# Three modulation vectors by a fused multiply and sum on VectorE instead of TensorE

## What is computed

```python
def adaln_params(cond, w_mod, b_mod):
    m = jax.nn.silu(cond) @ w_mod + b_mod
    return jnp.split(m[..., None, :], N_MOD, axis=-1)     # N_MOD = 6, w_mod [1024, 6144] per layer
...
        sh1, sc1, g1, sh2, sc2, g2 = adaln_params(c, w_mod[l], b_mod[l])
        csh1, csc1, cg1, csh2, csc2, cg2 = adaln_params(c_ctx, w_mod[l], b_mod[l])
...
        hf = modulate(rms_norm_2(x, norm_ffn[l]), sh2, sc2)
        x = x + g2 * conv_ffn(hf, w_up[l], conv_w[l], w_down[l])
```

## Time and profile before

| | us |
|---|---|
| median of 3 runs (lowest to highest) | 2077.11 (2076.71 to 2077.42) |
| span of the profiled execution | 2074.6 |
| PE busy | 2052.7 |
| DVE busy | 1367.3 |
| ACT busy | 1101.8 |

### The profile page before, as it was taken

One profiled execution on the slowest core, in us unless ns is written; L12 is line 12 of the kernel. 1 busy time (PEld: TensorE's weight loads), 2 busy tenths in 40 slices (PEclk: granted clock), 3 DMA queues, 4 the chain that ended last, 5 costly groups with the idle time before them and its releaser, 6 DMA issues.

```text
span 2074.6 us, 36374 instructions
## 1 busy us (share of the span) xinstructions
PE 2052.7 (99%) x14782; PEld 1832.1 (88%) x14782; DVE 1367.3 (66%) x2356; ACT 1101.8 (53%) x1839; POOL 72.2 (3%) x55
## 2 busy tenths in 40 slices
PE   9999999999999999999999999999999999999998
PEld 9999999999999999997677887778888888999998
DVE  6687767567687677574464445665555667667786
ACT  5576576545676685553476233433332346645554
POOL 2210000000300000000000000000000000000000
PEclk9999999999999999999999999999999999999999
DMA  8556444566655545564223434433333343454552
GB/s 286 180 166 207 160 143 166 190 218 235 226 170 187 176 130 183 201 221 158 82 72 102 152 129 176 142 112 132 112 132 127 117 152 107 140 180 161 186 174 81
DMA packets 93511, 330.62 MB, mean 159 GB/s; under 512 B 10272, under 2 KB 13600, under 8 KB 93088
## 3 DMA queue, kind: packets, MB, share of 16 engines
q1 hardware_dynamic: 93344, 328.30, 46.3%
HBM read 327.08 MB, written 1.18 MB: 158 GB/s over the span
## 4 chain that ended last, share of the span: by engine, by line
PE 91%; DVE 5%; ACT 3%; issue 1%; DMA 0%; DVEq 0%; SPq 0%; ACTq 0%
PE ps L945 25%; PE ps L946 24%; PE ps L947 24%; PE ps L1028 2%; PE ps L958 1%; PE ps L959 1%; PE ps L960 1%; DVE t_lo L1684 1%; ACT t_hi L1354 1%; PE ps L1259 1%; PE ps L1101 1%; PE ps L1269 1%; PE ps L1280 1%; PE ps L1117 1%; PE ps L1082 1%
## 5 line engine op out<-in xcount | busy, mean ns | idle before, releaser
L945 PE MATMUL ps<-t_RB,t_hi 128*128 128x256 f32 (+1 forms) x3712 | 1163.3, 313 | 4.0 <-ACT t_MT L1400 1.4
L946 PE MATMUL ps<-t_RB,t_hi 128*128 128x256 f32 (+1 forms) x3712 | 1144.2, 308 | 0.0
L947 PE MATMUL ps<-t_RB,t_lo 128*128 128x256 f32 (+1 forms) x3712 | 1143.7, 308 | 0.0
L1684 DVE TENSOR_TENSOR t_lo<-t_raw,t_hi 128x1024 fp32r<-128x1024 f32 (+1 forms) x503 | 608.7, 1224 | 355.5 <-ACT t_hi L1354 354.2
L945 PEld LDWEIGHTS ps<-t_RB,t_hi 128*128 128x128 f32 x3712 | 707.9, 191 | 74.7 <-issue 25.2
L946 PEld LDWEIGHTS ps<-t_RB,t_hi 128*128 128x128 f32 x3712 | 708.3, 191 | 35.0 <-issue 1.9
L947 PEld LDWEIGHTS ps<-t_RB,t_lo 128*128 128x128 f32 x3712 | 708.1, 191 | 35.2
L1354 ACT ACTIVATE t_hi<-t_raw 128x1024 fp32r<-128x1024 f32 (+1 forms) x506 | 520.4, 1041 | 398.7 <-PE ps L947 369.9
L2124 DVE SCALAR_TENSOR_TENSOR t_A<-ps,t_V,t_A 128x510 f32<-128x510 f32 (+1 forms) x176 | 102.1, 611 | 89.3 <-ACT t_A L1644 87.8
L1644 ACT ACTIVATE t_A<-ps,t_V 128x512 f32<-128x512 f32 (+1 forms) x88 | 48.4, 576 | 127.3 <-PE ps L947 127.3
L2097 DVE SCALAR_TENSOR_TENSOR t_X<-ps,t_MOD,t_X 128x256 f32<-128x256 f32 x168 | 72.6, 477 | 32.7 <-PE ps L947 32.7
(11 more groups left out here) (304 smaller groups left out, 1893.3 us busy)
## 6 DMA issues: line engine op xcount, KB each, us to landing
t_raw<-in_W SPq DMA_DIRECT2D x586, 512.0 KB, 3.8
t_A<-cu_scratch SPq DMA_DIRECT2D x8, 512.0 KB, 5.7
t_B<-cu_scratch SPq DMA_DIRECT2D x8, 512.0 KB, 5.6
t_raw<-in_W SPq DMA_DIRECT2D x16, 256.0 KB, 3.0
t_A<-in_C SPq DMA_DIRECT2D x2, 1536.0 KB, 6.9
t_X<-in_X SPq DMA_DIRECT2D x2, 512.0 KB, 4.3
t_X<-in_X SPq DMA_DIRECT2D x1, 1024.0 KB, 7.5
out<-t_X SPq DMA_DIRECT2D x4, 256.0 KB, 2.5
```

What stands on the lines that cost most here:

```text
L945: mm(o, hi[:, w], xh(k), start=k == 0 and j == 0, stop=False)
L946: mm(o, hi[:, w], xl(k), start=False, stop=False)
L947: i = mm(o, lo[:, w], xh(k), start=False, stop=k == nkt - 1 and m == u.x[1] - 1)
L1684: tt(t.lo[s][:, 0:w], t.raw[r][:, 0:w], t.hi[s][:, 0:w].bitcast(F), ALU.subtract).then_inc(*up("dve", ("split", u.i)))
```

## The change

For the second layer of the second block, the last three vectors (j = 3, 4, 5, in 24 pieces of 128 outputs, numbered 24 to 47) are no longer made on PE. A new unit `condb` loads the two conditionings, each copied to all 128 partitions, into `t.CB` (tiles `t_T1` and `t_E`), and ACT applies silu to them. A new unit `modv` takes one load of 128x1024, in which a partition holds the 1024 input weights of one output, and runs two fused instructions on DVE, one for each conditioning: multiply by the row of the conditioning, sum along the row from the bias on, and write the sum to a column of `t_MOD`. The product itself goes to the scratch `t.CBO` in the first and over the weights in the second. `modv` follows each of the first 24 weight products of the first feed-forward stage, and `condb` stands just before that stage. The list of vector units on PE is shorter by 12 (36 instead of 48); in the stage before it one follows every fourth product instead of every third, and in the feed-forward stage none. The other units keep their order. Left out of the diff are the tables that name the new functions, and the passing of the conditionings as an input.

```diff
@@ -131,6 +131,11 @@
         m = m[:, cols]
         return m.reshape(-1, 128, m.shape[1]).transpose(1, 0, 2).reshape(128, -1)
     return fn
+
+
+def outputs_by_rows(l, c):
+
+    return lambda inp: inp["w_mod_2"][l][:, 128 * c:128 * c + 128].T
 
 
 def small_cols(l):
...
@@ -167,7 +172,8 @@
         self.ng = self.ns = 0
         self.nn = [0, 0]
         self.turn, self.every, self.fine = 0, 0, False
-        self.mods, self.open = [(l, c) for l in range(L) for c in range(24)], []
+        self.mods, self.open = [(l, c) for l in range(L) for c in range(12 if l else 24)], []
+        self.rowmods = []
         self.width, self.late, self.sums = {}, [], {}
 
     def add(self, kind, **k):
...
@@ -246,6 +252,9 @@
 
     def mod_turn(self):
         self.turn += 1
+        if self.rowmods:
+            l, c = self.rowmods.pop(0)
+            self.add("modv", l=l, c=c)
         if self.every and self.turn % self.every == 0:
             self.some_mods(1)
 
...
@@ -545,7 +554,7 @@
         tw = 256 if last else 512
         nz = tw // 256
         t = 3 + 2 * l
-        self.every = 0 if last else 3
+        self.every = 0 if last else 4
         if last:
             self.need_mods(l, 1)
             self.add("s1", l=l, x=(1, t))
...
@@ -611,7 +620,9 @@
         b = self.rstd(t + 1, (2, 1, 1))
         self.add("norm2", l=t + 1, g=b, x=range(8))
         self.late_splits()
-        self.every = 0 if last else 3
+        if not last:
+            self.add("condb")
+            self.rowmods = [(1, c) for c in range(24, 48)]
 
         def down(g):
             nt = 4 if g else 2
...
@@ -638,7 +649,7 @@
         self.side.append(self.squares(t + 2, ((0, 1, 2, 3), (4, 5), (6,), (7,)) if last else ((0, 1, 2, 3), (4,), (5,), (6,), (7,))))
         down(5)
         self.drain()
-        self.every = 0
+        assert not self.rowmods
 
     def uf_chunk(self, l, c):
         return self.chunk(CH, wcols("w_in_2", l, 768 + np.arange(c * 256, c * 256 + 256)))
...
@@ -768,6 +779,7 @@
         low = CONST["swap1"][0]
         self.SS = [E[:, 0:512], E[:, 512:1024], E[:, 1024:1536], self.C1[:, low:low + 512],
                    self.C1[:, low + 512:low + 1024], self.T1[:, 768:1280], self.RS[:, :], self.SQA[:, :]]
+        self.CB, self.CBO = [self.T1[:, 0:1024], E[:, 0:1024]], a(4096, 1024)
         self.ident, self.ones = self.c1("ident"), self.c1("ones")
         self.S0 = [E[:, 512 * i:512 * i + 512] for i in range(3)] + [self.SQA[:, :]]
         self.PW = self.c2("poolw").rearrange("p (j l d) -> p j l d", j=2, l=2)
...
@@ -857,7 +869,7 @@
 
 def sync(e, units, t, M):
     q, up, at, was = Queue(e, M), M.up, M.at, M.was
-    rows = [(u, h) for u in units for h in range({"split": 1, "mod": 2}.get(u.kind, 0))]
+    rows = [(u, h) for u in units for h in range({"split": 1, "mod": 2, "modv": 1}.get(u.kind, 0))]
 
     def load(j):
 
...
@@ -865,7 +877,8 @@
             return
         if j >= NR:
             old, h = rows[j - NR]
-            q.wait_ge(at("split", old.i) if old.kind == "split" else at("modmm", old.l, old.c, h))
+            q.wait_ge(at("split", old.i) if old.kind == "split" else at("modv", old.l, old.c) if old.kind == "modv" else
+                      at("modmm", old.l, old.c, h))
         w = rows[j][0].x[0]
         e.dma_start(t.raw[j % NR][:, 0:w], t.d["W"][j, :, 0:w]).then_inc(*up(f"w{j % NR}", ("raw", j), by=16))
 
...
@@ -879,8 +892,13 @@
     e.dma_start(t.C1[:, 256:NC1], t.d["C1"][:, 256:NC1]).then_inc(*up("rest", ("rest",), by=16))
     for u in units:
         l, g = u.l, u.c
-        if u.kind in ("split", "mod"):
+        if u.kind in ("split", "mod", "modv"):
             load(u.x[1] + NR)
+        if u.kind == "condb":
+            q.wait_ge(at("pairmm", 0), at("n2h", 4, 5), at("n2l", 4, 5))
+            for z in range(2):
+                e.dma_start(t.CB[z], t.d["CB"][z:z + 1, :].to_broadcast([128, 1024])).then_inc(
+                    *up(f"cb{z}", ("cbraw", z), by=16))
         if u.kind == "mod":
             load(u.x[1] + 1 + NR)
         if u.kind == "small3":
...
@@ -1347,6 +1365,11 @@
         act(t.SM[:, 0:16], vec("cond", 0, 16), ACT.Silu).then_inc(*up("act", ("silu",)))
         q.wait_ge(at("silu"))
         act(t.C32[:, :, 0:2], t.cond, ACT.Copy).then_inc(*up("act", ("cond",)))
+
+    def condb(u):
+        for z in range(2):
+            q.wait_ge(at("cbraw", z))
+            act(t.CB[z], t.CB[z], ACT.Silu).then_inc(*up("act", ("condb",)))
 
     def split(u):
         s, r, w = u.i % NS, u.x[1] % NR, u.x[0]
...
@@ -1576,7 +1599,7 @@
             act(D[:, 256:512], ps[:, 256:512], ACT.Copy).then_inc(*up("act", ("rope2", u.l, w, m), ("gfree", u.g[0])))
 
     def k2(u):
-        q.wait_ge(at("downmm", 0, 5) if u.l else at("layer", 1))
+        q.wait_ge(*((at("downmm", 0, 5), at("modv", 1, 47)) if u.l else (at("layer", 1),)))
         rope2(u, "k", 0, gbank(u, 0)[:, :], t.K2)
 
     def v2(u):
...
@@ -1746,6 +1769,14 @@
         bias = vec("b_mod", l * 48 + 8 * j, 8).rearrange("p (q m) -> p q m", q=4).unsqueeze(3).to_broadcast([128, 4, 2, 2])
         q.wait_ge(at("modt", l, j))
         tt(o, ps, bias, ALU.add).then_inc(*up("dve", ("mod", l, j), ("sfree", u.s[0])))
+
+    def modv(u):
+        l, c, w = u.l, u.c, t.raw[u.x[1] % NR][:, :]
+        q.wait_ge(at("raw", u.x[1]), at("condb"), at("m2", 0), was("modv", l, c - 1))
+        for z in range(2):
+            e.tensor_tensor_reduce(out=w if z else t.CBO, in0=w, in1=t.CB[z], scale=1.0, scalar=vec("b_mod", l * 48 + c),
+                                   op0=ALU.mult, op1=ALU.add, accum_out=t.MOD[:, l * 96 + 2 * c + z:l * 96 + 2 * c + z + 1]).then_inc(
+                *up("dve", ("modv", l, c), ("mod", l, c // 8)))
 
     def small(u):
         b, l = t.gb[u.g[0] % 4], u.l
...
@@ -2211,6 +2242,9 @@
             u.x, r = (HF, len(rows)), u.c % 4
             fn = wcols("w_mod_2", u.l, np.arange(u.c // 4 * 1024, u.c // 4 * 1024 + 1024), np.arange(256 * r, 256 * r + 256))
             rows += [(fn, h, HF) for h in range(2)]
+        elif u.kind == "modv":
+            u.x = (HF, len(rows))
+            rows.append((outputs_by_rows(u.l, u.c), 0, HF))
         units.append(u)
     return units, rows
 
```

6 lines of the change are left out of this document (3 added, 3 removed).

## The result

The changed kernel takes 2080.4 us (median of 17 runs, 2077.56 to 2083.32) against 2077.37 for the kernel before in the same session (17 runs). Forecast were 2070.2 us and a range that ended at 2076. The prediction was wrong. In all comparisons single executions at a much lower clock are left out (one of the kernel before at 2487 us, one of e7_fill at 3327 us).

A forecast was written before the change was run, and what follows sets the result against it. TensorE, busy 2052.7 of 2074.6 us, was taken to bound the kernel. Terms: -17.7 + 1.0 + 1.5 + 8.3 = -6.9, a span of 2067.7 and, 2.5 above it, 2070.2 us; range 2060 to 2076.

The forecast's parts named there:

- The mechanism of the gain: On TensorE: vector units, transposes and a bank wait come off its time, 17.7 us, while VectorE has room for the pairs.
- first rival: In the stage: VectorE's room hides all pairs, no bank comes late, only the norm's unit costs; -16.7, 2060.4 us; 17%.
- The fused instruction: On VectorE in the stage: about 1.20 us a step, 2.40 a pair, busy time 1.28; 24 pairs are 58 us.
- The rival that it takes twice as long with both operands in SBUF: VectorE's fused instruction takes twice as long a column; a pair 4.5 us, in sum +17.4, 2094.5 us; 10%.
- The opening: Start of the stage: silu of the late-landing conditionings delays freeing a bank; TensorE waits 1.5 us, between 0 and 4.3.
- The first down group: In the stage: pairs in VectorE's queue delay banks; TensorE waits twice, 8.3 us in all, between 6.8 and 9.5.
- So 13 go from places where TensorE never waits: 13 x 1.20 = 15.6.: On TensorE: 12 units leave the list and one moves into the norm behind the stage, each saving 1.20 us.
- The wait of 1.43: TensorE's bank wait at the first down group, held by a vector unit's copy behind the glu; goes, saving 1.4 us.
- the walk of the queue: VectorE's queue at the first down group, written out on the old clock: two waits, 2.1 and 5.2 us, together 7.3.
- The fourth unit at the norm: Norm behind the stage: four units stand instead of three, costing 1.0 us, between 0.4 and 1.4.
- the weights are no more than before: Loads for the fused pairs in the stage: 24 loads for 24, so no added cost.
- the three waits that it forecast: TensorE waits of 1.5 us at the stage's opening and two at the first down group, 8.3 us in all.

The follow-up runs named there:

- e7_fill: Changed kernel with dummy products on TensorE ahead of three of its waits, other work unchanged: 2077.67 us, ratio 1.0 to the kernel before.
- e6_best: e4_all with the third pair's glu one turn later and one vector unit at the norm behind the stage moved between sum and broadcast: 2061.65 us, ratio 0.9929.
- e4_all: Changed kernel with the edits of e1_front3 and e2_later together: 2066.32 us, ratio 0.9944 to the kernel before.
- e9_narrow: e6_best with each fused instruction working on 32 of the 1024 columns, loads and waits between engines kept: 2061.66 us, ratio 0.9924.
- e1_front3: Changed kernel with the vector units ahead of the stage on every third turn again instead of every fourth: 2076.22 us, ratio 0.9988.
- e2_later: Changed kernel with condb behind the first pair of up products and the first modv behind the first group of down products: 2071.0 us, ratio 0.9965.
- e10_condb_open: Changed kernel with the first fused pair behind the first down group, conditionings still loaded at the opening of the stage: 2075.89 us, ratio 0.999.
- e8_noidle: Kernel before without the dummy products at the norms ahead of and behind the stage: 2078.81 us, ratio 1.0006.
- e11_double: Changed kernel with every fused instruction done twice, 96 in place of 48: 2118.73 us, ratio 1.0201 to the kernel before.
- e3_onemod: Changed kernel with one of four vector units at the norm behind the stage moved among the up products: 2078.59 us, ratio 1.0004.

## Why the prediction was wrong

**The mechanism of the gain was right.** TensorE bounds the kernel, the vector units come off its time, the pairs fit beside it: e6_best, with the 12 units gone and no new wait in the stage, is 15.5 us faster than the kernel before of its session. The prediction's first rival had put the gain at 16.7; that it came near is luck, since this kernel has another spacing, the pairs later and the glu moved as well (e4_all, without the two last edits, saves 11.2).

**The fused instruction** was sized right: 1.28 us busy, a step of 1.21, a pair 2.41 (1370.38, 1371.59 and 1372.80 below). The rival that it takes twice as long with both operands in SBUF is refuted. The Trainium skill says in Vector Engine (DVE) Microarchitecture Reference, section Points that are easy to get wrong, that two sources in SBUF that are not bf16 halve the rate of its scalar-tensor-tensor form; this fused form takes 1.04 ns a column ((1280 - 248) / 992, from e9_narrow), and the plain subtraction, from 691 ns for 512 columns to 1245 for 1024 in the changed kernel, 1.08. So no run here shows the halving for this form, and the measurement decides.

**The opening** was right in mechanism: silu of the second conditioning ended at 1317.66, 3.59 us less on the old clock is 1314.1 (forecast 1313.2, bounds 1311 to 1315), and the wait was 2.3 us (forecast 1.5, bounds 0 to 4.3). The two copies took 7.0 and 7.8 us to land. Timeline, ScalarE, of the changed kernel:

```profile
...
1316.60 1.06 ACT L1372 ACTIVATE t_E<-t_E 128x1024 f32<-128x1024 f32 x1 [0.21 <-DMA t_E<-in_CB]
...
```

**The first down group** was right in its two places and its order, the second half's first bank and the first bank of the up products behind it, and none later: 2.68 and 3.29 us. That is 6.0 where 8.3 was forecast (6.8 to 9.5); in e1_front3, where the clock stays full between the two, it is 2.68 + 4.92 = 7.6. VectorE's queue there (a pair ahead of the first emptyings, and behind the glu a pair ahead of those of the second half):

```profile
...
1370.38 1.28 DVE L1777 CUSTOM_DVE_ANT_0 t_A<-t_raw,t_T,t_V 128x1024 f32<-128x1024 f32 x1
...
1371.59 0.08 DVE L1777 DVE_READ_ACCUMULATOR2_ANT t_MOD<- 128x1 f32 x1
...
1372.80 0.08 DVE L1777 DVE_READ_ACCUMULATOR2_ANT t_MOD<- 128x1 f32 x1
...
1381.06 1.28 DVE L1777 CUSTOM_DVE_ANT_0 t_A<-t_raw,t_T,t_V 128x1024 f32<-128x1024 f32 x1
...
1383.46 0.08 DVE L1777 DVE_READ_ACCUMULATOR2_ANT t_MOD<- 128x1 f32 x1
...
```

The prediction had the first emptying at 1368.3; it came at 1372.80. TensorE was late by as much (its first half ended at 1371.0 instead of 1367.0), because of what had happened ahead of the stage and at its opening.

Three steps failed.

**1. "So 13 go from places where TensorE never waits: 13 x 1.20 = 15.6."** This was false for two of them. Ahead of the transposes at 1027.70, which wait 1.52 us in the kernel before, a unit stood at 1020.87 that the new spacing moves away; the wait grew to 2.20, so 0.5 of the unit's 1.20 us came off. The wait of 1.43 had a unit in front of it as well, and is 2.58 in e2_later, e4_all and e10_condb_open. I had read rightly that the bank was held up by the unit's copy on ScalarE behind the glu, and concluded that the wait goes with the unit, a gain of 1.4 us. It does not: without the unit the next bank is emptied behind the same glu, on VectorE. In the sum the walk of the queue made up for that, in the first rival nothing did. Only the stage was read for waits. The stretch ahead of it, where two units go, was never looked at, though the diff changes a number there.

**2. The fourth unit at the norm: "+1.0, between 0.4 and 1.4".** It was 6.2. The bounds came from the norm ahead of the stage, where four units stand too. But there the loads come in time. A ring of seven slots holds the loads, they are issued in order, and behind the stage the fourth unit's stand behind one whose slot comes free only with a split that VectorE does just ahead of the small steps (SP's issues and VectorE, of the changed kernel):

```profile
...
1673.90 7.34 SPq L883 DMA_DIRECT2D t_raw<-in_W  x9
...
```

```profile
...
1672.65 1.22 DVE L1707 TENSOR_TENSOR t_lo<-t_raw,t_hi 128x1024 fp32r<-128x1024 f32 x1 [1.35 <-ACT t_hi L1377]
...
1680.92 0.42 DVE L1763 TENSOR_TENSOR t_MT<-t_MT,ps 128x256 f32<-128x256 f32 x1 [6.19 <-PE ps L1046]
1681.26 1.65 DVE L2027 SCALAR_TENSOR_TENSOR t_E<-t_X,t_S1S,ps 128x256 f32<-128x256 f32 x4
...
```

The split starts at 1672.65, the issues behind it start at 1673.90, and the unit's two halves wait until 1677.14 and 1679.77. VectorE has nothing to do in that time: the addition of this unit, which stands ahead of the norm in its queue, starts at 1680.92 after 6.19 us of idling for TensorE. In the kernel before the issues there start as late (1673.83), and nobody wanted those loads yet. The prediction said that the weights are no more than before, and left it there; when they can be issued was not asked.

**3. What was left out: the clock behind a wait.** The sum priced each wait at its own length. The windows of before show a granted clock of 1.00 from 900 to 1700, and I took it for a constant. In the changed kernel's runs 7 us more of clock are lost than before in the mean (11.9 to 4.7); in the two profiled executions 12.2 more, up to 1700 us. e7_fill shows that activity in the waits brings it back, and e8_noidle that idleness in the kernel before takes it away. Not every low stretch is the change's doing: the one at 927 stands ahead of all of it. The Trainium skill says in TensorE: Matmul & The Clock Gate, section HAM oscillation — how this bites in real kernels, that an engine left idle by waits is throttled to half its clock and starts the next products cold; the runs here agree, and show it behind waits as short as 0.89 and 2.20 us. Had the prediction priced this at 1.7 us a wait (half of the 3.4 us from 1374.5 to 1377.9) for each of the three waits that it forecast, it would have come to 2075.3 us. That is hindsight, and too simple: behind the opening wait no clock was lost.

Against the 13.7 us between forecast and profile stand, by the table: 0.9 by the front's longer wait and its first 0.2, 5.2 by the norm, 1.0 in the rest, and 8.8 of lost clock up to the norm (1.8 of it at 927), less 2 because the waits in the stage came out 1.5 shorter than forecast and the one ahead of the small step 0.5 shorter than before. By the medians the gap is 10.2, and what part each has there is not shown: the places of the low clock differ from run to run.

## What to carry to other kernels

Before work is taken off the bounding engine, look at each piece for a wait in the next few microseconds behind it, on that engine: a piece that stands in front of a wait is paid for already, and removing it mostly lengthens the wait (here by 0.7 and by 1.2 of its 1.2 us). A diff's one-number change of spacing moves such pieces at places far from the work it is about. And where an engine's clock depends on its being busy, a wait costs more than its length if the engine sets the pace behind it; what does not remove a wait can at least fill it. Last, one profile is one execution: before two of them are subtracted, compare the stretch in which both kernels do the same work.

## What the runs showed of the hardware

How long a wait must be for the clock to fall is not settled by its length alone. At the wait of 1028, 2.20 us were followed by the lower clock in all six kernels that had it (granted 0.57 to 0.80 in the 8 us behind it), and 1.52 us in none of six. At 927, where all kernels have done the same work, waits of 0.88 us and less were followed by 1.00 in all nine profiles that have them, and those of 0.89, 0.90, 0.91 and 0.97 by 0.79. But 2.58 us at the first down group were followed by 1.00 in e2_later and e4_all and by 0.79 in e10_condb_open; in e11_double 2.38 and 3.76 us (at 1535 and 1550) were followed by 1.00, and 2.38 us at 1463 by 0.80; and the same wait of 2.68 us at the first down group was followed by 0.79 in the changed kernel and by 1.00 in e1_front3 and e3_onemod. The opening waits of 1.46 to 2.29 us (five profiles) were all followed by 1.00, the one of 2.68 us (e11_double) by 0.79, and at the norm of e6_best 0.66 us by 0.80.

The kernel before has it too, seldom. Of 58 of its runs beside these experiments, the 16 with a mean granted clock of 0.999 took 2076.8 us in the mean, and the 8 with 0.996 took 2081.4. The times of these 58 runs, from 2076.33 to 2083.05 us, so go with the granted clock.

A fused multiply and sum of 128x1024 in fp32 with both operands in SBUF takes 1.28 us and one of 32 columns 0.25; it is hardly slower than a plain subtraction of that size (1.22 to 1.24).
